# Two one-hot tables of a gate product, moved from VectorE to GpSimd and ScalarE

## What is computed

```python
sv, si = lax.top_k(scores, PEER_TOPK)
cand = sv[..., 0, :, None] + sv[..., 1, None, :]
cv, ci = lax.top_k(cand.reshape(t, PEER_HEADS, PEER_TOPK * PEER_TOPK), PEER_TOPK)
i1 = jnp.take_along_axis(si[..., 0, :], ci // PEER_TOPK, axis=-1)
i2 = jnp.take_along_axis(si[..., 1, :], ci % PEER_TOPK, axis=-1)
experts = (i1 * PEER_NKEYS + i2).reshape(t, PEER_HEADS * PEER_TOPK)
gates = jax.nn.softmax(cv, axis=-1).reshape(t, PEER_HEADS * PEER_TOPK)
...
act = jax.nn.gelu(jnp.einsum('tkd,td->tk', expert_u[eb], xb, preferred_element_type=jnp.float32))
return jnp.einsum('tk,tkd->td', act * gb, expert_v[eb].astype(jnp.float32)).astype(xb.dtype)
```

## Time and profile before

| | us |
|---|---|
| three runs, median | 5057.75 |
| three runs, lowest and highest | 5054.53, 5059.38 |
| the profiled execution, time | 5062.22 |
| the profiled execution, span of the core | 5060.4 |
| PE busy | 4256.8 |
| DVE busy | 2735.3 |
| ACT busy | 1446.5 |
| POOL busy | 593.9 |

### The profile page before, as it was taken

How to read it: one execution, slowest core, us unless ns; L and a number is a source line. 1 busy time by engine, 2 the same in 40 slices (tenths; PEclk the granted TensorE clock), 3 DMA queues, 4 the chain that set the end, 5 groups by cost and what they waited for, 6 DMA issues and landing times. The chain is left out here.

```text
span 5060.4 us, 52602 instructions
## 1 busy us (share of the span) xinstructions
PE 4256.8 (84%) x20559; PEld 3569.1 (71%) x20559; DVE 2735.3 (54%) x4312; ACT 1446.5 (29%) x2204; POOL 593.9 (12%) x393
## 2 busy tenths in 40 slices
PE   7995794579889899999879878598998977767998
PEld 5883693468888799999758635377877854446886
DVE  3223674549998876777632256644333225665343
ACT  2221222323233333333222115233222211613322
POOL 0000001000555563333100000000000000000000
PEclk8997896789899999999989978799999987878999
DMA  3442004333678689999634310132323421022232
GB/s 109 143 141 84 1 1 129 109 108 119 206 249 309 233 277 324 335 347 349 224 100 143 103 59 1 36 133 75 100 91 110 141 80 59 1 71 98 92 99 77
DMA packets 333850, 691.47 MB, mean 137 GB/s; under 512 B 24067, under 2 KB 89091, under 8 KB 332332
## 3 DMA queue, kind: packets, MB, share of 16 engines
q1 hardware_dynamic: 256380, 466.98, 28.4%
q0 software_dynamic: 36864, 134.23, 7.7%
q10 hardware_dynamic: 40368, 87.04, 4.5%
HBM read 583.04 MB, written 105.14 MB: 136 GB/s over the span
## 5 line engine op out<-in xcount | busy, mean ns | idle before, releaser
L310 DVE TENSOR_TENSOR in_w_low<-in_w,in_w_high 128x512 fp32r<-128x512 f32 x344 | 214.5, 686 | 650.8 <-ACT in_w_high L304 650.8
L354 PE MATMUL ps<-xn_high,in_w_high 128*128 128x512 f32 x1056 | 414.7, 393 | 51.0 <-DVE in_w_low L310 51.0
L1699 PE MATMUL ps<-xn_p_high,pe_w_high 128*128 128x384 f32 (+1 forms) x1152 | 411.4, 357 | 46.2 <-DVE pe_w_low L1872 46.2
L354 PE MATMUL ps<-xn_high,in_w_low 128*128 128x512 f32 x1056 | 414.1, 392 | 0.0
L354 PE MATMUL ps<-xn_low,in_w_high 128*128 128x512 f32 x1056 | 413.6, 392 | 0.0
L1699 PE MATMUL ps<-xn_p_high,pe_w_low 128*128 128x384 f32 (+1 forms) x1152 | 401.0, 348 | 0.0
L1699 PE MATMUL ps<-xn_p_low,pe_w_high 128*128 128x384 f32 (+1 forms) x1152 | 400.2, 347 | 0.0
L1872 DVE TENSOR_TENSOR pe_w_low<-pe_w_raw,pe_w_high 128x2048 fp32r<-128x2048 f32 x136 | 329.9, 2427 | 106.1 <-ACT pe_w_high L1806 105.7
L1806 ACT CAST pe_w_high<-pe_w_raw 128x2048 fp32r<-128x2048 f32 x136 | 259.4, 1909 | 419.0 <-DMA pe_w_raw<-in_peer_v 223.7
L310 DVE TENSOR_TENSOR mlp_w_low<-mlp_w,mlp_w_high 128x512 fp32r<-128x512 f32 x256 | 159.7, 686 | 369.1 <-ACT mlp_w_high L304 369.1
L1729 PE MATMUL ps<-pe_far_hidden_high,pe_w_high 128*128 128x384 f32 x1024 | 346.0, 338 | 14.1 <-DVE pe_near_hl L1999 13.9
(11 more groups left out here) (533 smaller groups left out, 9282.0 us busy)
## 6 DMA issues: line engine op xcount, KB each, us to landing
in_w<-in_w_in SPq DMA_DIRECT2D x86, 1024.0 KB, 6.1
pe_w_raw<-in_peer_uT SPq DMA_DIRECT2D x64, 1024.0 KB
pe_w_raw<-in_peer_v SPq DMA_DIRECT2D x64, 1024.0 KB
dram_pf<-in_out ACTq DMA_DIRECT2D x33, 1024.0 KB, 8.3
mlp_w<-in_w_up SPq DMA_DIRECT2D x32, 1024.0 KB, 5.3
mlp_w<-in_w_down SPq DMA_DIRECT2D x32, 1024.0 KB, 5.0
dram_peer_hidden<-pe_rings_r ACTq DMA_DIRECT2D x64, 384.0 KB
dram_peer_gates<-pe_near_gate_out SPq DMA_DIRECT2D x6, 4096.0 KB, 17.9
```

What stands on the lines that cost most here:

```text
L310: dve.tensor_tensor(lo[:, s, c, :], raw[:, s, c, :], hi[:, s, c, :].bitcast(F32), ALU.subtract).then_inc(lo_done, 1)
L354: last = pe.matmul(k.ps[:, 4 * parity + q, :], a, b, start=(i == 0 and c == 0 and p == 0), stop=(i == upg - 1 and c == UC - 1 and p == 2))
L1699: last = pe.matmul(ps[:, q, 0:n], w[:, s, at], xp[:, 4 * i + c, 0:n], start=(i == 0 and c == 0 and p == 0), stop=(i == 1 and c == 3 and p ...
```

## The change

VectorE's `gates` goes. GpSimd writes `I` directly: per token one instruction compares `iota` with the token's first key and multiplies by its gate, both taken as one value per partition. ScalarE writes `J`: per token the distance |key - iota|, then over the 8 tokens of a step the positive part of 1 - distance. The semaphore `one_i` goes, `away` comes between ScalarE's two stages, and GpSimd and ScalarE now wait for `kept_T` and `gate_made` themselves. The due times are `GATE` - 2 and + 1 on ScalarE, + 1 and + 3 on GpSimd (before: + 0 and + 2 on VectorE, + 2 and + 4 on GpSimd).

```diff
+                def ones_j():
+                    for it in range(n_gates):
+                        yield GATE(it) - 2.0
+                        s = it % RING
+                        if it % 16 == 0:
+                            act.wait_ge(kept_T, 2 * (TURNED.index(it // 16) + 1))
+                        if it >= RING:
+                            act.wait_ge(gate_made, 2 * (it - RING + 1))
+                        for j in range(UNIT):
+                            t = it * UNIT + j
+                            last = act.activation(J[s][:, j, :], iota[:, :], ACT.Abs, bias=keyT[:, 1, t:t + 1], scale=-1.0)
+                        last.then_inc(away, 1)
+                        yield GATE(it) + 1.0
+                        act.wait_ge(away, it + 1)
+                        act.activation(J[s], J[s], ACT.Relu, bias=1.0, scale=-1.0).then_inc(one_j, 1)
...
-                def gates():
-                    full = [P, UNIT, P]
-                    for it in range(n_gates):
-                        yield GATE(it)
-                        s = it % RING
-                        dve.wait_ge(kept_T, 2 * (TURNED.index(it // 16) + 1))
-                        if it >= RING:
-                            dve.wait_ge(gate_made, 2 * (it - RING + 1))
-                        for c, to, done in ((0, I_[s], one_i), (1, J[s], one_j)):
-                            if c == 1:
-                                yield GATE(it) + 2.0
-                            keys = keyT[:, c, it * UNIT:(it + 1) * UNIT]
-                            dve.tensor_tensor(to, iota[:, :].unsqueeze(1).to_broadcast(full), keys.unsqueeze(2).to_broadcast(full),
-                                              ALU.is_equal).then_inc(done, 1)
...
                     for it in range(n_gates):
                         for o in range(2):
-                            yield GATE(it) + 2.0 + 2.0 * o
+                            yield GATE(it) + 1.0 + 2.0 * o
                             if o == 0:
-                                pool.wait_ge(one_i, it + 1)
-                            n = 2 * it + o
-                            to = I_[it % RING][:, 4 * o:4 * o + 4, :]
-                            pool.tensor_tensor(to, to, gateT[:, 4 * n:4 * n + 4].unsqueeze(2).to_broadcast([P, 4, P]),
-                                               ALU.mult).then_inc(gated, 1)
+                                pool.wait_ge(kept_T, 2 * (TURNED.index(it // 16) + 1))
+                                if it >= RING:
+                                    pool.wait_ge(gate_made, 2 * (it - RING + 1))
+                            for j in range(4 * o, 4 * o + 4):
+                                t = it * UNIT + j
+                                last = pool.tensor_scalar(I_[it % RING][:, j, :], iota[:, :], keyT[:, 0, t:t + 1], gateT[:, t:t + 1],
+                                                          ALU.is_equal, ALU.mult)
+                            last.then_inc(gated, 1)
```

More of the change, by code:

```diff
@@ L1584, in peer @@
                                                                            "turned", "kept_T"))
-    one_i, one_j, gated, gate_made, gate_kept, gate_stored = (sem(n) for n in ("one_i", "one_j", "gated", "gate_made",
+    away, one_j, gated, gate_made, gate_kept, gate_stored = (sem(n) for n in ("away", "one_j", "gated", "gate_made",
                                                                                "gate_kept", "gate_stored"))
@@ L1862, in raise_sparse @@
                     act.activation(act_s[:, :], act_s[:, :], ACT.Gelu_apprx_tanh).then_inc(act_raised, 1)
-                weave(split(), x_copies(), evictions(), softmax(), gates(), raise_sparse(), hidden_high())
+                weave(split(), x_copies(), evictions(), softmax(), gates(), ones_j(), raise_sparse(), hidden_high())
             @block.vector
@@ L2040, in rows_of_experts @@
                             dve.scalar_tensor_tensor(acc[:, :], rows[s], share[:, j:j + 1], acc[:, :], ALU.mult, ALU.add).then_inc(row_used, 1)
-                weave(split(), join(), route(), choose(), gates(), rows_of_experts(), hidden_split(), totals())
+                weave(split(), join(), route(), choose(), rows_of_experts(), hidden_split(), totals())
             @block.gpsimd
```

## The result

| | us |
|---|---|
| after, median of 4 runs (lowest, highest) | 5195.98 (5186.34, 5200.56) |
| before, median of 4 runs on the same chip (lowest, highest) | 5058.57 (5054.53, 5067.14) |
| ratio, 95% interval | 1.0267 (1.0247 to 1.0287) |
| the profiled execution after: span | 5184.5 |

The account below looks back on a forecast made before the run. VectorE's queue was taken as the bound in the two routing stretches. 38 + 9 - 17 = 30 us off the profiled 5062.2 gave 5032; as that execution lay 4.5 above the median, 5028 us, 8 in 10 from 4985 to 5100.

Parts of the forecast that it names:

- the price of the small instruction: GpSimd's compare and multiply on 128x128 taken as 0.35 us alone, between 0.20 and 0.57.
- Turns: GpSimd's waits for VectorE's two-input instructions: 2.2 us per step, 0.27 us for each of 8, effective price 0.62 us.
- The sum over a burst: GpSimd has 8.4 us of work per 8.0 us step, drops behind about 3 us per burst, recovers in the pause.
- Rival 2: GpSimd's in-order queue becomes the bound from an effective 0.91 us; at 1.02 it costs 41 us, 5099; chance 0.20.
- For both routing stretches I take back 38: In 1420:1500 and 1620:1700, relieving VectorE and the new order return 38 of PE's 55.0 lost us.
- The store stretches, 9: Around the gate table's 4 MB store, PE no longer waits for `J` and gating: 4.5 us at two places, 9 together.
- ScalarE charged nothing: ScalarE's added 4.3 us per step, 204 us in all, costs no time, since `J` is planned 8 units ahead.
- Rival 1: Turns between GpSimd's 384 small instructions and VectorE eat nearly all of the 30 us, within 10 of 5058; chance 0.13.
- Rival 3: PE hardly waits any more: at a small instruction near 0.20 us, 70 of 83.6 us return, 4988; chance 0.13.
- rival 4: The change does nothing, `J` and `I` waiting for the same late thing elsewhere: 5058, within the first rival's 0.13.
- the mean above 0.9: Sign that the forecast is wrong: GpSimd's small instructions average above 0.9 us, where 0.6 was expected.
- The clock near 1.00: Sign that the forecast is right: PE's granted clock near 1.00 in both routing stretches.

Follow-up runs that it names:

- cheap_i: The change with the compare in GpSimd's small instruction replaced by a multiplication; 5087.64 us, 1.0056 against the kernel before.
- i_on_pool: The kernel before with only `I` moved to GpSimd's 384 small instructions, `J` staying on VectorE; 5235.64 us, 1.0346 against the kernel before.
- no_dots: The change with VectorE's dot products of the sparse rows each replaced by a copy of one column; 5121.42 us, 1.0106 against the kernel before.
- half_i: The change with half of GpSimd's small instructions left out, 4 instead of 8 per step; 5059.63 us, 0.9994 against the kernel before.
- j_on_act: The kernel before with only `J` moved to ScalarE, `I` made on VectorE and gated on GpSimd; 5055.78 us, 0.999 against the kernel before.
- fused_dve: The change with `I` made on VectorE by one compare-and-gate instruction per token, GpSimd gating nothing; 5029.2 us, 0.9933 against the kernel before.

## Why the prediction was wrong

- **The term that failed first: the price of the small instruction**, "one pass at the pace of the multiplication", 0.35 us. It is 0.78 alone, above the upper bound of 0.57. That bound was two passes of a multiplication, and the step assumed that a compare goes at a multiplication's pace. cheap_i, which differs from the change in that alone, recovers 112 of the 137 us.
- **Turns**, 0.27 us per instruction, were 1153 - 780 = 373 ns on average, and 804 - 430 = 374 in cheap_i at little more than half the price. For 8 that is 3.0 us per step, about half of the 5.6 us that L1889 and the dots take there (120.7 and 147.2 us in 1330:2050 of the change's trace, over 48 steps). The effective 0.62 became 1.15.
- **The sum over a burst held**, once it has these sizes. The prediction let GpSimd drop behind by what its work exceeds 8.0 us per step, 8 times per burst, less 8 us of lead, six times. With the mean durations of each trace for 8 small instructions and 2 gathers, and nothing taken back, that is an estimate of 128 us for the change (11.67 us of work per step; 137 measured by the medians), 171 for i_on_pool (12.56; 173), 56 for no_dots (10.17; 57), none for half_i (7.96; none). Only cheap_i's 26 us are not in it (8.93 us of work, none by the sum). The estimate is made after the fact, from durations that already hold the turns. With the forecast's prices the step was 8.4 us.
- **Rival 2 was right in kind**: GpSimd's in-order queue bounds the burst, from the first one. Its break-even counted the pause as time that GpSimd can use: (94.4 - 36)/64. It can't: its order holds no gate step there (in the change none between 1429.8 and 1453.3), and the gathers wait for dots (79.9 us in all). A second estimate, of the whole burst, with a step of 8 small instructions and 2 gathers, each 0.17 us from its neighbour, times 8, plus the pause of 18: after 8 x (9.22 + 2.45 + 0.34) + 18 = 114 us per burst, no_dots 8 x (7.83 + 2.34 + 0.34) + 18 = 102. Scaled from 94.4 by the steps' whole time (560.9, 684.4 and 606.7 us) they took 115 and 102. By this estimate the break-even is ((94.4 - 18) / 8 - 2.8) / 8 = 0.84 us, not 0.91. For cheap_i it gives 92, and 97 were measured; that remainder I can't assign.
- **"For both routing stretches I take back 38"**: j_on_act and half_i relieve VectorE without the loss, and PE still waited 9.73 and 9.57 us there in the one, 6.84 and 8.02 in the other. The new order puts half of `I` ahead of the gather, but the dot-gather chain remained. The reading of the earlier trace rows was right as to who is late, except that it took the 6.56 us of L1948 for its price, where 4.3 are a turn with GpSimd; that a relief of VectorE by 3 us per step would be enough was wrong.
- **The store stretches, 9**: in fused_dve one wait of 5.61 us is left there, for L1860. ScalarE's Relu stands behind the cast that waited 11.53 us for its weights. So `J` on ScalarE changes queues but stays behind the same late load.
- **ScalarE charged nothing**: no run speaks against it, j_on_act least of all (0.999). Eight Abs took 2.44 us and the Relu 1.06, 3.5 us per step instead of 4.3. The estimate of 3.6 from the Trainium skill, "ScalarE: Activation LUTs", section "What ACT_TABLE_LOAD costs", was the nearer one. VectorE's L1889 does wait longer for L1806, 242.3 us in 46 waits against 64.8 in 21 before, and PE's matmuls waited 15.9 us for L1860. Both were named as signs of a ScalarE that is late; but half_i has 212.3 and 16.9 us of them and no loss. That an emptier VectorE merely comes earlier to the same cast fits this and isn't shown by itself.
- **Rival 1**, turns eat the gain: they are real, 384 x 0.37 = 142 us of GpSimd's 440, and made the loss larger; but they did not stop at eating the gain, and at the price of 0.78 GpSimd was short of time without the dots too. VectorE's side of them did not cost more than before: a dot took 1235 ns on average against 1313, and L1889 2464 against the 2687 of L1872 before. Rival 3 fell. So did rival 4 for the change, but j_on_act and half_i, at 0.999 and 0.9994, came out as it says, though not for its reason: the late thing was the dot in front of the gather, not the weights.
- Of the signs named in advance, the mean above 0.9 and PE waiting for `I` in the first burst came true, and so did the two of ScalarE just told. The clock near 1.00 did not: it was 0.84 and 0.94 in the two routing stretches. DVE under 62 us in both routing stretches came true as well (52.60 and 39.25) and proved nothing, since the whole phase had slowed down.

## What to carry to other kernels

Before work goes to another engine, price the exact operation there, not its shape: a two-line series of eight instructions would have shown 0.78 us. Count an in-order queue over the burst in which its work is due, not over burst and pause. Where two chains end within a few microseconds of each other, each cut alone can measure as next to nothing, as here: test them together. And before an instruction's long duration is taken for its price, look at what the other engine does beside it.

## What the runs showed of the hardware

- GpSimd's price depends on the operation: 128x128 in fp32 took 0.58 us for a compare, 0.78 with a multiplication behind it, 0.43 for two multiplications. VectorE does compare and multiply in 0.28 (four in 1.11 us).
- That instruction of VectorE has one tensor input, but it isn't free of turns. In fused_dve's trace, four of them stand for 6.10 us beside GpSimd's multiplication of 4.58. GpSimd's timeline, then VectorE's:

```profile
1458.64 4.58 POOL L2064 TENSOR_TENSOR pe_far_rest<-pe_far_rest,pe_far_sif 128x2048 f32<-128x2048 f32 x1
```

```profile
1457.72 6.10 DVE L1999 TENSOR_SCALAR pe_near_I<-pe_iota,pe_key_T,pe_gate_T 128x128 f32<-128x128 f32 x4
```

- The Trainium skill, "SBUF — State Buffer", section "Who interferes with whom", says that `tensor_scalar` can enter a mode with two ports and then contends with GpSimd, whoever is first holding the pair for a whole instruction. By that rule the trace agrees: 6.10 us instead of 1.11. Who came first the records don't show: the dot that was held for 6.02 us in half_i is recorded from 1466.13, GpSimd's multiplication from 1466.45.
- Several two-input instructions of VectorE in a row let GpSimd through hardly at all: 4.2 of their 5.1 us were added to four small instructions (5.96 against 1.75).
